# Retention heads overlapped: the output product of one head around the value product of the next

## The reference, cut to what matters

```
q, k, v, g = split(x @ w_in)              # k scaled by 1/16, q and k rotated for the 256 live tokens
a = (q k^T) * decay(i - j)                # forward decay below the diagonal, backward above,
                                          # context tokens enter with both
o = a @ v
o = (o - mean(o)) * rsqrt(var(o) + EPS) * gn_g[head]
y += (silu(g) * o) @ w_out[512 * head : 512 * (head + 1)]
```

## Time and profile before

| | |
|---|---|
| runs | 3654.14 us median of 3 (3653.74 to 3654.33) |
| the profiled execution's own time | 3641.96 us |
| its span, first to last instruction | 3640.2 us |
| mean granted TensorE clock | 0.973 |
| TensorE busy | 3426.0 us, 94% |
| VectorE, ScalarE, GpSimd busy | 1837.8, 1429.1, 116.5 us |
| DMA | 498.21 MB, mean 137 GB/s |

### The profile page before, as it was taken

The page is one execution under the profiler, slowest core; times in us unless marked ns, Lnnn a source line. Parts: engine busy times, 40 slices in busy tenths (PEclk is TensorE's granted clock), DMA queues, the critical chain, the costliest instruction groups (busy, mean ns, idle before and its releaser), DMA issues.

```text
span 3640.2 us, 44790 instructions
## 1 busy us (share of the span) xinstructions
PE 3426.0 (94%) x18006; PEld 2849.6 (78%) x18006; DVE 1837.8 (50%) x2604; ACT 1429.1 (39%) x1906; POOL 116.5 (3%) x159
## 2 busy tenths in 40 slices
PE   7999979999999789999999999979999999999998
PEld 6888758888888678878887666858887888887797
DVE  6756766757656767543324333353323333334654
ACT  5545435545444445442223222232223222242443
POOL 0000000000000000000000000000000000032000
PEclk9999989999999999999999999989999999999999
DMA  7854426848644348632323122212231323253254
GB/s 251 266 169 158 141 83 229 266 164 272 229 146 142 127 144 266 216 104 93 113 85 110 58 70 70 93 44 96 93 110 64 116 93 99 92 139 58 71 185 151
DMA packets 355416, 498.21 MB, mean 137 GB/s; under 512 B 13170, under 2 KB 224012, under 8 KB 355212
## 3 DMA queue, kind: packets, MB, share of 16 engines
q1 hardware_dynamic: 351052, 483.76, 40.5%
q0 software_dynamic: 4160, 11.59, 1.6%
HBM read 494.21 MB, written 1.10 MB: 136 GB/s over the span
## 4 chain that ended last, share of the span: by engine, by line
PE 86%; DVE 7%; ACT 4%; issue 2%; POOL 1%; DMA 0%; SPq 0%; DVEq 0%; POOLq 0%; ACTq 0%
PE bank L474 26%; PE bank L475 25%; PE bank L476 25%; PE bank L487 2%; PE bank L489 2%; ACT xn L983 1%; DVE wlo L1312 1%; PE bank L874 1%; PE bank L849 1%; PE bank L893 1%; PE bank L599 1%; POOL small L2001 1%; ACT xTh L989 1%; PE bank L878 1%; ACT whi L938 0%
## 5 line engine op out<-in xcount | busy, mean ns | idle before, releaser
L1312 DVE TENSOR_TENSOR wlo<-raw,whi 128x1024 fp32r<-128x1024 f32 (+1 forms) x926 | 1107.2, 1213 | 1318.5 <-ACT whi L938 1317.1
L938 ACT ACTIVATE whi<-raw 128x1024 fp32r<-128x1024 f32 (+1 forms) x926 | 951.4, 1048 | 1234.5 <-PE bank L476 1190.1
L474 PE MATMUL bank<-xTh,whi 128*128 128x256 f32 (+1 forms) x3200 | 1047.2, 327 | 21.6 <-DVE xTl L1367 19.0
L475 PE MATMUL bank<-xTl,whi 128*128 128x256 f32 (+1 forms) x3200 | 1040.7, 325 | 0.0
L476 PE MATMUL bank<-xTh,wlo 128*128 128x256 f32 (+1 forms) x3200 | 1040.1, 325 | 0.0
L474 PEld LDWEIGHTS bank<-xTh,whi 128*128 128x128 f32 x3200 | 609.5, 190 | 95.7 <-DVE xTl L1367 27.5
L475 PEld LDWEIGHTS bank<-xTl,whi 128*128 128x128 f32 x3200 | 609.7, 191 | 50.3
L476 PEld LDWEIGHTS bank<-xTh,wlo 128*128 128x128 f32 x3200 | 609.4, 190 | 48.9
L474 PE MATMUL bank<-whi,hh 128*128 128x512 f32 x968 | 381.9, 395 | 18.5 <-DVE hl L1447 18.5
L475 PE MATMUL bank<-wlo,hh 128*128 128x512 f32 x968 | 380.1, 393 | 0.0
L476 PE MATMUL bank<-whi,hl 128*128 128x512 f32 x968 | 380.1, 393 | 0.0
(11 more groups left out here) (329 smaller groups left out, 2644.4 us busy)
## 6 DMA issues: line engine op xcount, KB each, us to landing
raw<-in_ffn_w_in_dram SPq DMA_DIRECT2D x176, 1024.0 KB, 5.1
raw<-in_ffn_w_out_dram SPq DMA_DIRECT2D x80, 1024.0 KB, 5.1
raw<-in_w_mod_dram SPq DMA_DIRECT2D x72, 1024.0 KB, 5.2
raw<-in_w_in_dram SPq DMA_DIRECT2D x44, 1024.0 KB, 5.1
raw<-in_ret_w_in_dram SPq DMA_DIRECT2D x24, 1024.0 KB, 5.1
raw<-in_w_branch_dram SPq DMA_DIRECT2D x12, 1024.0 KB, 5.0
raw<-in_nat_w_qkv_dram SPq DMA_DIRECT2D x12, 1024.0 KB, 6.7
raw<-in_ffn_w_out_dram SPq DMA_DIRECT2D x16, 512.0 KB, 3.5
```

The source lines that it names most:

```text
L474: pe.matmul(ps, lh, rh, start=start, stop=False, skip_group_check=True)
L475: pe.matmul(ps, lh, rl, start=False, stop=False, skip_group_check=True)
L938: nc.scalar.activation(hi, src, ACT.Copy).then_inc(*e.inc("hi", key, part))
L1312: nc.vector.tensor_tensor(lo, src, hi.bitcast(F32), ALU.subtract).then_inc(*e.inc("lo", key, part))
```

## The change

The order of the work on the three engines and of the slabs is rewritten; the arithmetic is the same, and so are the buffers and the number of instructions of each kind.

- PE: head 0 ends after its scores. Head 1 is q, the value product of head 0, k, the transposes of head 0, v, g, scores of head 1. From head 1 on, the scores are followed by the first half of the output product of the head before, the value product of this head, the second half of the output product of the head before, and the transposes of this head. After head 3 both halves of its own output product follow.
- Slabs: ("rw", h-1, 0) and ("rw", h-1, 1) stand behind g of head h; those of head 3 behind them.
- DVE: the normalisation issues the statistics of tile t before it waits for the power of tile t-1. Before it stand the splits up to `ahead_of_tail` of the second half's slab, behind it one more split, the rows of the second half, and the low parts of the transposed result.
- ACT: the same order for its part; one more split ("rw", h-1, 1 part 1) stands before the exponentials of the decay weights. Head 0's rows go to Y in head 1.

```diff
-        for n in range(2):
-            s.add(("rw", h, n), rows(w["ret_w_out_2"][0], 4 * h, 4, 512 * n, 512), 4, 512)
+        for g in ([h - 1] if h else []) + ([3] if h == 3 else []):
+            for n in range(2):
+                s.add(("rw", g, n), rows(w["ret_w_out_2"][0], 4 * g, 4, 512 * n, 512), 4, 512)
...
+            def read_out(h, n):
+                if n == 0:
+                    pe.wait_ge(*e.at("yT", ("r", h), 3))
+                token_major([("rw", h, n)], ("rwp", h, n), range(4), rYh, rYl, by_tile=int(h == 3 and n == 1))
+
+            for h in range(4):
+                queries_or_keys("q", h)
+                if h == 1:
+                    retained(0)
+                queries_or_keys("k", h)
+                if h == 1:
+                    turn_y(("r", 0), rg, 4, 512, ("ry", 0))
+                for part in "vg":
+                    token_major([(("r" + part, h), 0), (("r" + part, h), 1)], ("r" + part + "p", h),
+                                range(4), *xT[512])
+                scores(h)
+                if h:
+                    read_out(h - 1, 0)
+                    retained(h)
+                    read_out(h - 1, 1)
+                    turn_y(("r", h), rg, 4, 512, ("ry", h))
+            for n in range(2):
+                read_out(3, n)
...
             for h in range(4):
...
+                kept("q", rq, h)
+                kept("k", rk, h)
+                if h == 1:
+                    turned_out(0)
...
                 if h:
+                    until(slabs.part_index[("rw", h - 1, 1), 1])
                     act.wait_ge(*e.at("ra", h - 1, 2))
...
+                if h == 1:
+                    first_rows(0)
+                if h:
+                    ahead_of_tail(until, ("rw", h - 1, 1))
+                    ahead(until, ("rw", h - 1, 1))
+                if h == 1:
+                    first_rows(1)
+                if h:
+                    turned_out(h)
+            ahead(until, ("rw", 3, 0))
+            first_squares(("g2", 0), 512)
+            ahead_of_tail(until, ("rw", 3, 1))
...
+            def normalised(h):
+                for t in range(5):
+                    if t < 4:
+                        o = 144 + 16 * (t % 2)
+                        dve.wait_ge(*e.at("rop", h, t))
+                        link(V.bn_stats(small[:, o:o + 6], unit("rop", h, t)[:, :]))
+                        link(V.bn_aggr(small[:, o + 6:o + 8], small[:, o:o + 6]))
+                        TS(small[:, o + 7:o + 8], small[:, o + 7:o + 8], EPS, None, ALU.add).then_inc(*e.inc("ms", ("ro", h, t)))
+                    if t:
+                        o = 144 + 16 * ((t - 1) % 2)
+                        dve.wait_ge(*e.at("rstd", ("ro", h, t - 1)))
+                        m = TS(rt[:, (t - 1) % 2, :], unit("rop", h, t - 1)[:, :], small[:, o + 6:o + 7], small[:, o + 8:o + 9],
+                               ALU.subtract, ALU.mult)
+                        m.then_inc(*e.inc("rn", h, t - 1, frees=("rop", h, t - 1)))
+                        dve.wait_ge(*e.at("rn", h, t - 1))
+                        dve.wait_ge(*e.at("rg", h, t - 1))
+                        TT(rg[:, t - 1, :], rg[:, t - 1, :], rt[:, (t - 1) % 2, :], ALU.mult).then_inc(*e.inc("ry", h, t - 1))
...
+            for h in range(4):
+                rotated("q", rq, h)
+                if h == 1:
+                    normalised(0)
+                rotated("k", rk, h)
+                if h == 1:
+                    turned_out(0)
+                for half in range(2):
+                    ahead(until, (("rv", h), half))
+                decays(h)
+                for half in range(2):
+                    ahead(until, (("rg", h), half))
+                if h:
+                    until(slabs.part_index[("rw", h - 1, 1), 1])
+                weights(h)
+                if h > 1:
+                    for t in range(4):
+                        row(h - 1, t, 0)
+                if h:
+                    ahead_of_tail(until, ("rw", h - 1, 1))
+                    normalised(h)
+                    ahead(until, ("rw", h - 1, 1))
+                    for t in range(4 if h > 1 else 0):
+                        row(h - 1, t, 1)
+                    turned_out(h)
```

More of the change, by code:

```diff
@@ L818, in _, with queries_or_keys, scores @@
             turn_in(("r",), 512, ("xn", ("r",)))
[L819 to L825, removed]
+            def queries_or_keys(part, h):
+                feature_major(("r" + part, h), 512, [("r" + part + "p", h, i) for i in range(2)], *xT[512],
+                              norm=("r",) if h == 0 and part == "q" else None)
+            def scores(h):
                 pe.wait_ge(*e.at("rqk", h))
@@ L1209, in _, with kept, turned_out, first_rows @@
             turned(("r",), 512, gain2, bias2(0, 1))
-            for h in range(4):
[L1211 to L1217, removed]
+            dist = rcst[:, R_DIST:R_DIST + 512].rearrange("p (j i) -> p j i", j=2)
+            act.wait_ge(*e.at("lg"))
+            def kept(part, dst, h):
+                ahead(until, ("r" + part, h))
+                for i in range(2):
+                    act.wait_ge(*e.at("r" + part + "p", h, i))
+                    if h:
+                        act.wait_ge(*e.at("rap", h - 1, 2))
+                    A(dst[:, i, 256:512], unit("r" + part + "p", h, i)[:, 256:512], ACT.Copy).then_inc(*e.inc("r" + part + "c", h, i))
+            def turned_out(h):
+                turned_y(("r", h), 4, 512, rYh, lambda c: col(1, GN + 4 * h + c))
+            def first_rows(n):
+                for t in range(4):
+                    act.wait_ge(*e.at("rwp", 0, n, t))
+                    A(stripe(Y, n, t), unit("rwp", 0, n, t)[:, :], ACT.Copy).then_inc(*e.inc("Y0", n, t, frees=("rwp", 0, n, t)))
+            for h in range(4):
+                kept("q", rq, h)
+                kept("k", rk, h)
+                if h == 1:
+                    turned_out(0)
                 for half in range(2):
@@ L1856, in _, with rotated, decays @@
             dve.wait_ge(L.sem("rcst_landed"), 16)
[L1857 to L1878, removed]
+            def rotated(part, dst, h):
+                ahead(until, ("r" + part, h))
+                p0, p1 = (unit("r" + part + "p", h, i)[:, 0:256] for i in range(2))
+                for i in range(2):
+                    dve.wait_ge(*e.at("r" + part + "c", h, i))
+                if h:
+                    dve.wait_ge(*e.at("rap", h - 1, 2))
+                r0, r1 = rt[:, 0, 0:256], rt[:, 0, 256:512]
+                TT(dst[:, 0, 0:256], p0, cosT, ALU.mult)
+                TT(r0, p1, sinT, ALU.mult)
+                TT(dst[:, 1, 0:256], p1, cosT, ALU.mult)
+                link(TT(r1, p0, sinT, ALU.mult))
+                TT(dst[:, 0, 0:256], dst[:, 0, 0:256], r0, ALU.subtract)
+                m = TT(dst[:, 1, 0:256], dst[:, 1, 0:256], r1, ALU.add)
+                m.then_inc(*e.inc("rope", h, part, also=[("rqk", h)], frees=("r" + part + "p", h, 0)))
+                L.freed[("r" + part + "p", h, 1)] = L.events[("rope", h, part)]
+                dve.wait_ge(*e.at("rope", h, part))
+            def decays(h):
                 if h:
@@ L1884, in _, with weights @@
                 TT(WX[:, :, 1, :], WX[:, :, 1, :], wtmp[:, :, 1, :], ALU.add).then_inc(*e.inc("wlog", h))
+            def weights(h):
                 dve.wait_ge(*e.at("wexp", h))
@@ L1923, in _ @@
-                for n in range(2):
-                    if h == 3 and n == 1:
-                        ahead_of_tail(until, ("rw", h, n))
-                        first_squares(("g2", 0), 512)
-                    else:
-                        ahead(until, ("rw", h, n))
-                        for t in range(4 if h else 0):
-                            rows(t, n)
+            def normalised(h):
[15 more added lines that the diff above has]
+                        TT(rg[:, t - 1, :], rg[:, t - 1, :], rt[:, (t - 1) % 2, :], ALU.mult).then_inc(*e.inc("ry", h, t - 1))
@@ L1931, in _ @@
+            ahead(until, ("rw", 3, 0))
+            for t in range(4):
+                rows(t, 0)
+            ahead_of_tail(until, ("rw", 3, 1))
+            first_squares(("g2", 0), 512)
             rows = block_two_ffn("g2", 0, 2, 512, (0, 1), ("g1", 1), rows)
```

60 lines of the change are left out of this document (18 added, 42 removed).

## The result

The changed kernel ran in 3594.78 us (median of 4, 3591.85 to 3599.61), the kernel before in 3654.23 (median of 4, 3653.74 to 3654.33): ratio 0.9845, 95% interval 0.983 to 0.986, 59.5 us less. The profiled execution of the changed kernel took 3591.85 us, that of before 3641.96, 50.1 less. The two differences, 59.5 and 50.1, do not agree, and that turned out to be the point.

What follows compares the result with a forecast made beforehand. TensorE, busy 94%, bounds the kernel, so only its waits and half clock in the heads can be won: 33.5 + 6.7 + 8.2 less 1.2 and 1.4 is 45.8 us, giving profiled 3596.2, median 3608.3, range 3602 to 3615.

Steps and rivals of the forecast that it cites:

- The sum itself: All terms together: 33.5 + 6.7 + 8.2 = 48.4 us saved, less 1.2 and 1.4 for new waits, is 45.8.
- Before the value product: In the heads, PE's 1.52 us wait for the weighted scores ra was to go, behind 48 output matmuls (10.9 us).
- Before the transposes: In the heads, PE's waits for normalised rows rg (2.89 and 2.88 us in head 1) were to go, 4.4 to spare.
- Pipelining the normalisation: DVE's normalisation chain in the heads: costed at nothing when covered; without cover, less than 3.3 us a head.
- Before the output product: PE's wait for low parts rYl (1.63 us in head 1): gone in heads 0 to 2, staying in head 3.
- The bank wait: New wait in head 1: v needs banks of k until DVE has rotated k; 1.2 us once, bounds 0 and 2.9.
- The clock at head 3: Half clock after head 3's one remaining wait, some 2.9 us: costs nothing or 2.9 us, middle 1.4 taken.
- Heads 1 and 2: Between first score matmuls of heads 2 and 3: 87.05 + 17.32 = 104.4 us at a clock of 1.00.
- Half clock remaining: Rival: the short waits at heads 1 and 3 each leave PE at half clock, 2.9 us each; 3612.7 us, chance 0.12.
- Partly covered: Rival: DVE starts the normalisation late, PE waits at the transposes, 2 us in each of three heads; 3614.3 us, chance 0.08.
- Slower: Rival: a split or bank release behind DVE's normalisation holds PE in heads 1 to 3; 3672 us, chance 0.02.
- no effect: Rival: the waits return elsewhere in full with the same clock loss; 3654 us, chance 0.03.

Runs made afterwards that it cites:

- r1: The kernel before, copied without any edit: median 3648.2 us of 12 runs, 3641.55 to 3652.81.
- r2: The changed kernel, copied without any edit: 3604.04 us (4 runs, 3598.84 to 3606.44), ratio 0.9876 to the kernel before.
- r9: The changed kernel with both halves of the previous head's output product behind the value product, heads 1 to 3: 3608.00 us, one execution.
- r6: The changed kernel with both halves of the previous head's output product ahead of the value product, heads 1 to 3: 3620.93 us, one execution.
- r5: The changed kernel with DVE's split of the first part of the next k ahead of the normalisation, heads 1 to 3: 3624.23 us, one execution.
- r3: The changed kernel with the normalisation loop of before, tile by tile without pipelining: 3595.32 us (4 runs, 3591.65 to 3600.39).
- r4: The kernel before with only the normalisation pipelined by a tile: median 3642.1 us, ratio 0.9988 (interval 0.9974 to 1.0002).
- r7: The changed kernel with the transposes of head 0 moved behind the value projection v of head 1: 3606.74 us, one execution.

## Why the prediction was wrong, point by point

**The step that failed** is the one from the profiled execution to the runs: "The profiled execution took 3641.96, the median of the runs is 3654.14, 12.2 more; I carry that difference." I took 12.2 us as something that belongs to the runs, because three of them agreed to 0.6 us. It does not: the median lies 2.9 us above the profiled execution for the changed kernel (3594.78 and 3591.85), 3.3 us below it in r1 and 0.3 below in r2. With 55 runs before's mean is 5 us lower, and both kernels reach over 14 us. What held before's first four runs within 0.6 us stays open; of the 51 later ones only 5 lie between 3653.7 and 3654.5. Of the 13.6 us by which the forecast missed, 9.3 are this carried difference; the other 4.3 are 1.8 of the sum, treated next, 2.4 ahead of the heads and 0.1 behind them. The 0.2%, 7.3 us, that I gave as what a measurement can tell was too small as well: the medians of four moved by 8 and 9 us without an edit. The runs of after that the forecast was measured against were 4.8 us below that kernel's own mean of 12, the runs of before 5.1 above theirs: 9.9 of the 59.5 us are this spread, 49.5 the change as the pooled runs have it. The range of 13 us was drawn for the clock behind the heads; the trace shows no spread there (1217.1 to 1217.5 us), and all of it ahead of them. With half of the spread of 14 us added at its lower end, 3602 less 7, it would have reached 3595, where the result is.

**The sum itself** came out at 45.8 us against 47.6 in the trace.
- Before the value product: covered, as said. r9 takes the cover away and the wait is back, at 2.48 us with the extra split that I had bounded at 2.4 and that measures 1.0.
- Before the transposes: covered. I gave it 4.4 us to spare; DVE ends at 2232.5 in head 2 (below), 16.0 us after the value product begins, where PE needs it after 21.2, so 5.2. r6 and r5 show what is behind that.
- Pipelining the normalisation: nothing under the cover, as said (r3). Without the cover I had allowed up to 3.3 us a head, and the expectation of r4 2.4; it is 0.8, since the first two tiles are bound by PE.
- Before the output product: gone in heads 0 to 2, left in head 3. From the first transpose to the first output matmul it is 2346.28 - 2342.06 = 4.22 us there, where I kept 4.67: the transposes are faster at full clock.
- The bank wait: 1.33 us where 1.2 was worked out, and r7 shows the cause by removing it.
- The clock at head 3: 1.4 us was a middle between nothing and 2.9. It is 0 in the three profiles of the changed kernel, and 1.6 in r7. That nothing was lost is in part luck: the waits of the same 2.31 us in the part ahead of the heads let the clock fall at 436 us in eleven of thirteen profiles and at 1205 us in eight.
- Heads 1 and 2: 104.3 us against 104.4.

DVE in head 2 of the changed kernel, the first statistics and the last product:

```profile
2220.20 0.70 DVE L1937 BATCH_NORM_STATS2 small<-bank 128x6 f32<-128x512 f32 x1 [0.47 <-PE bank L851]
...
2231.85 0.69 DVE L1948 TENSOR_TENSOR rg<-rg,rt 128x512 f32<-128x512 f32 x1
```

The other terms' errors are tenths; the 1.8 us between 45.8 and 47.6 is the clock term (1.4) and the 0.45 of the last transposes, less 0.1 of the bank wait.

**The rivals.** Half clock remaining did not happen in the changed kernel: 1.33 us and 2.31 us left it at 1.00 in all three profiles. The sentence of the Trainium skill that I set against it ("TensorE: Matmul & The Clock Gate", "A second HAM failure mode: psum-queue depth-cycling") is not refuted by this: in r7 the clock fell after 2.31 us, in r9 after 2.48. After 1.33 us no profile here shows a fall. Partly covered did not happen either, but r5 shows how near it is: one split. Slower and no effect are excluded.

## What to carry to other kernels

Cover each wait with the work that fits it: the first half of a product for a short wait ahead, the second for the long one behind. On an engine that works through its queue in order, what stands ahead of the covered chain decides, and one split that can only be done late cost 8 us a head. And before a difference of a few tenths of a per cent between a profile and a few runs is carried into a forecast, see from several executions whether it belongs to the program or to the one execution; marks at the edges of the changed stage compare two profiles to 0.1 us where the runs are 14 us apart.

## What the runs showed of the hardware

Executions of the same program on one core differ by up to 14 us in 3650, 0.4%. Between two profiles of before the two large steps lie in stages where TensorE's clock differs, 0.94 and 0.75 from 496 to 557 us and 0.97 and 0.93 from 1149 to 1216 us. At 500 to 510 us it is 1.00 in one execution and 0.50 in the other, with 57 and 42 matmuls. The Trainium skill ("TensorE: Matmul & The Clock Gate", "What's actually happening") says that the number of matmuls at the slow clock differs from run to run of one kernel, and that the slow start costs less than 1% of a typical kernel's span. The runs here agree that it differs and stay below that size, but the differences lie in the middle of the kernel and not at its start.

After a wait of 1.33 us (for rk) or 1.52 us (for ra) the clock stayed at 1.00 in every profile here that has one. After 2.31 us in head 3 it stayed in the three profiles of the changed kernel and in r3 and fell in r7 and r9. With the waits of that length at 436 and 1205 us in all thirteen profiles, it stayed after 11 of 32 and fell after 21. After 2.48 us it fell in two of three heads of r9. A fall in r7 cost 1.6 us, after head 1 of before 2.9.
